# Dealing anew how many expert rows and routing heads stand beside each stage of a hybrid encoder layer

## The reference

```
proj = x @ w_in                       # q, k, v | latents of the second attention | two gates
o_a  = stick_breaking_attend(...)     # first attention ("stick"), 8 heads of 64
o_b  = mla_attend(...)                # second attention ("mla"), 8 heads
h = layer_norm(ALPHA * x + (sig(g_a) * (o_a @ w_oa) + sig(g_b) * (o_b @ w_ob)) @ w_out)
# PEER, for each token:
q = (h @ peer_wq).reshape(8 heads, 2, 128)
s1, i1 = top_k(q0 @ sub_keys0, 16);  s2, i2 = top_k(q1 @ sub_keys1, 16)
top_s, experts = top_k(s1[:, None] + s2[None, :], 16)      # out of 16384 experts
ff = sum over 8 heads x 16 picks of  softmax(top_s) * gelu(u[e] . h) * v[e]
y = layer_norm(ALPHA * h + ff)
```

## Time and profile before

| | |
|---|---|
| median of 3 runs | 3386.64 us |
| profiled execution, and its span | 3386.37 us, 3384.6 us |
| TensorE (PE) matmul busy | 2957.3 us, 87% |
| VectorE (DVE) busy | 2398.4 us, 71% |
| GpSimd (POOL) busy | 1548.0 us, 46% |
| ScalarE (ACT) busy | 1204.6 us, 36% |
| DMA | 1096.91 MB, mean 324 GB/s |

### The profile page before, as it was taken

One profiled execution on the slowest core, in us unless ns is written; L12 is line 12 of the kernel. 1 busy time (PEld: TensorE's weight loads), 2 busy tenths in 40 slices (PEclk: granted clock), 3 DMA queues, 4 the chain that ended last, 5 costly groups with the idle time before them and its releaser, 6 DMA issues. The chain is left out here.

```text
span 3384.6 us, 35758 instructions
## 1 busy us (share of the span) xinstructions
PE 2957.3 (87%) x10191; PEld 1649.7 (49%) x10191; DVE 2398.4 (71%) x4846; ACT 1204.6 (36%) x3117; POOL 1548.0 (46%) x1180
## 2 busy tenths in 40 slices
PE   8989989766697998876788899999989999999993
PEld 5755655443444555433444555544444545545551
DVE  0121477787777867887767777777778787888887
ACT  0241233474633434775653332222222222322221
POOL 0000066655664677876878643323333333333330
PEclk9978999887798999897799999999999999999996
DMA  4566699868699999557689999999999999999994
GB/s 148 192 247 203 215 337 336 310 220 273 226 357 389 385 337 348 157 176 221 173 280 329 334 388 416 415 415 415 415 416 415 415 414 415 410 408 413 415 407 178
DMA packets 374853, 1096.91 MB, mean 324 GB/s; under 512 B 91616, under 2 KB 209344, under 8 KB 288512
## 3 DMA queue, kind: packets, MB, share of 16 engines
q0 software_dynamic: 164784, 750.26, 58.7%
q1 hardware_dynamic: 176800, 303.85, 25.3%
q10 hardware_dynamic: 33072, 40.51, 3.4%
HBM read 1031.18 MB, written 62.23 MB: 323 GB/s over the span
## 5 line engine op out<-in xcount | busy, mean ns | idle before, releaser
L459 POOL DMA_INDIRECT expert_rows<-in_experts,picked_index x525 | 620.7, 1182 | 881.9 <-DVE ff_sum L613 756.2
L601 DVE SCALAR_TENSOR_TENSOR expert_rows<-expert_rows,h_tile 128x1024 f32<-128x1024 f32 x557 | 679.3, 1220 | 236.1 <-DMA expert_rows<-in_experts,picked_index 217.6
L482 POOL DMA_INDIRECT gates_by_expert<-dense_gate,gate_address x384 | 680.7, 1773 | 164.0 <-issue 116.5
L1829 PE MATMUL dense_out_ps<-dense_value_rows,dense_weights 128*128 128x512 f32 x1536 | 697.1, 604 | 63.4 <-DVE dense_weights L1907 63.4
L613 DVE SCALAR_TENSOR_TENSOR ff_sum<-expert_rows,coefficients,ff_sum 128x1024 f32<-128x1024 f32 x557 | 712.9, 1280 | 29.3 <-ACT coefficients L564 28.1
L1840 PE MATMUL dense_act_ps<-dense_hT,key_columns 128*128 128x384 f32 x2048 | 683.1, 487 | 5.8 <-issue 3.5
L1840 PEld LDWEIGHTS dense_act_ps<-dense_hT,key_columns 128*128 128x128 f32 x2048 | 389.1, 190 | 306.7 <-issue 55.9
L1829 PEld LDWEIGHTS dense_out_ps<-dense_value_rows,dense_weights 128*128 128x128 f32 x1536 | 294.8, 193 | 422.7 <-issue 314.7
L870 PE MATMUL proj_ps<-xT,w_in_block 128*128 128x384 f32 (+1 forms) x1392 | 421.8, 466 | 29.2 <-PEq L1640 16.1
L558 ACT ACTIVATE activated<-dots 128x1 f32<-128x1 f32 (+1 forms) x629 | 125.9, 200 | 883.6 <-DVE expert_rows L601 653.1
L870 PEld LDWEIGHTS proj_ps<-xT,w_in_block 128*128 128x128 f32 x1392 | 268.0, 193 | 182.4 <-issue 35.6
(11 more groups left out here) (199 smaller groups left out, 3228.2 us busy)
## 6 DMA issues: line engine op xcount, KB each, us to landing
key_columns<-in_key_columns SPq DMA_DIRECT2D x128, 512.0 KB
dense_value_rows<-in_experts SPq DMA_DIRECT2D x128, 512.0 KB
gates_by_expert<-zeros POOLq DMA_DIRECT2D x12, 2048.0 KB, 21.9
wq_half<-in_peer_wq SPq DMA_DIRECT2D x48, 512.0 KB
dense_gates<-gates_by_expert SPq DMA_DIRECT2D x128, 192.0 KB
w_in_block<-in_w_in ACTq DMA_DIRECT2D x18, 1024.0 KB
w_in_block<-in_w_in SPq DMA_DIRECT2D x18, 1024.0 KB
w_out<-in_w_out SPq DMA_DIRECT2D x24, 512.0 KB, 7.2
```

The lines of the kernel that those rows point to most:

```text
L459: pool.indirect_dma_start(to, None, self.a["experts"], bass.IndirectOffsetOnAxis(ap=index[:, k:k + 1], axis=0)).then_inc(got, 16)
L482: pool.indirect_dma_start(self.a["gates_by_expert"], bass.IndirectOffsetOnAxis(ap=self.flat[i][:, k:k + 1], axis=0), self.dgate[i][:, k:k ...
L601: dve.scalar_tensor_tensor(place, place, 1.0, self.h[n % 2][:], ALU.mult, ALU.mult, accum_out=self.dots[:, s % TOPK:s % TOPK + 1]).then_in ...
L1829: mm = nc.tensor.matmul(out[d][:, 512 * half:512 * (half + 1)], w[e % AB][:, P * d:P * (d + 1)], vals[e % VB][:, 512 * half:512 * (half + ...
```

## The change

Only the numbers of `SHARES` change. The work of the program as a whole is the same: 689 row steps, 66 heads of routing, 384 scatters.

```diff
-        ((1, "project"), 44, 1, 7, 44), ((1, "stick"), 24, 2, 2, 24), ((1, "mla_project"), 8, 1, 1, 10), ((1, "mla"), 22, 2, 2, 24),
-        ((1, "merge"), 22, 1, 0, 20), ((1, "scores"), 27, 1, 3, 16),
-        ((2, "project"), 39, 1, 8, 56), ((2, "stick"), 28, 2, 5, 60), ((2, "mla_project"), 7, 1, 1, 20), ((2, "mla"), 25, 2, 5, 56),
-        ((2, "merge"), 16, 1, 2, 34), ((2, "scores"), 28, 1, 3, 30),
+        ((1, "project"), 36, 1, 9, 50), ((1, "stick"), 29, 2, 0, 30), ((1, "mla_project"), 10, 1, 0, 10), ((1, "mla"), 22, 2, 2, 24),
+        ((1, "merge"), 22, 1, 1, 16), ((1, "scores"), 27, 1, 3, 16),
+        ((2, "project"), 34, 1, 11, 58), ((2, "stick"), 36, 2, 1, 58), ((2, "mla_project"), 7, 1, 1, 20), ((2, "mla"), 30, 2, 3, 54),
+        ((2, "merge"), 14, 1, 4, 34), ((2, "scores"), 26, 1, 4, 34),
```

## The result

| | before | after |
|---|---|---|
| median, same chip | 3385.57 us (9 runs, 3380.03 to 3390.80) | 3401.42 us (9 runs, 3394.80 to 3409.49) |
| ratio | | 1.0039, 95% interval 1.0029 to 1.0050 |
| profiled span | 3384.6 us | 3398.8 us |
| TensorE, VectorE, GpSimd busy | 2957.3, 2398.4, 1548.0 us | 2950.1, 2403.6, 1538.1 us |

The account below looks back on a forecast made before the run. Bounds were taken by block: TensorE and DMA in projections, GpSimd in stick 2 to mla 2, DMA in dense. Terms -8 -1 -1 +0 +1.5 +1 -4 +3.5 +2 -3 = -9 gave 3377.5 us; own range 3368 to 3384, overall 3352 to 3400.

Parts of the forecast that it names:

- The projections: Project 1 -8 us (-12 to -3), barrier wait 14.5 to some 6.5; project 2 +1 (-3 to +7).
- Stick 1: Stick 1, 5 rows more and 2 heads fewer: -1 us, between -5 and +4; VectorE +12 - 14.
- mla_project 1 at -1 and mla 1 at 0: mla_project 1: -1 us (-3 to +3); mla 1 keeps its shares: 0 (-2 to +2 together with scores 1).
- The three blocks -4: Stick 2, mla_project 2 and mla 2 together, bound by GpSimd: -4 us, between -12 and +6.
- its -3 for both blocks: GpSimd's work over stick 2 and mla 2, from fetches, scatters and score loads: about -3 us in all.
- VectorE's -11: VectorE's work: stick 2 -8.8 us and mla 2 -2, expected to be given back in good part.
- ScalarE's tables: Stick 2: gelu table loads taken as covered; the rival has them bind, +10.3 us on ScalarE's path, 3393 total; chance 0.04.
- Merge 2 at +3.5: Merge 2, 2 rows fewer and 2 heads more: +3.5 us, between 0 and +9; VectorE 4 late in the seventh step.
- Scores 2 at +2: Scores 2, 2 rows fewer and 1 head more around the wait for tile 5's scores: +2 us, -3 to +8.
- Dense at -3: Dense: 3 rows fewer -7.6 us, late scatters +5 (0 to +18); in all -3, between -8 and +10.
- The rival of the freeze: Dense: a stop of 25 us from late scatters isn't made up, dense +17, 3398 total; chance 0.12.
- GpSimd takes the attentions' gain: Rival: GpSimd's scatter backlog runs from stick 2 to mla 2, +5 us instead of -4, 3386.5 total; chance 0.08.

Follow-up runs that it names:

- e5_rows25: e3_even with 25 row steps in mla 2 in place of 30, dense taking the 5: 3386.98 us, ratio 0.9985.
- e9_rows_only: The changed kernel with 25 row steps in mla 2 in place of 30, heads kept, dense taking the 5: 3381.62 us, ratio 1.0000.
- e6_mlap: The changed kernel with mla_project 1's old shares (8 row steps, 1 head, the head taken from merge 1): 3398.36 us, ratio 1.0024.
- e11_two_fixes: The changed kernel with the edits of e6_mlap and e9_rows_only together: 3377.26 us, ratio 0.9977.
- e3_even: The changed kernel with group 2's same rows but its heads spread as 10, 4, 1, 4, 2, 3: 3401.10 us, ratio 1.0033.
- e10_scatters: e3_even with 42 scatters allowed in mla 2 in place of 54: 3397.73 us, ratio 1.0039.
- e4_gates: The changed kernel with 60 scatters allowed in scores 2 in place of 34, so none is left for dense: 3415.38 us, ratio 1.0071.
- e13_stick_rows: The changed kernel with 24 row steps in stick 1 in place of 29, dense taking the 5: 3385.09 us, ratio 1.0008.
- e8_combined: Against the changed kernel: group 1 as e6_mlap; group 2 keeps the new deal only in projection and stick: 3375.90 us, ratio 0.9966.
- e7_gates1: The changed kernel with group 1's old numbers of scatters allowed, rows and heads kept: 3394.05 us, ratio 1.0016.

## Why the prediction was wrong

The forecast was a sum of -9 with its steps by block; +14.2 came. By its own steps:

- **The projections: right.** -8 for project 1 and +1 for project 2, with the tail of one piece as what remains. TensorE's wait at the barrier fell from 14.5 to 6.7, where 6.5 was forecast, and project 2 kept its 6.6, with 8 us more of VectorE's work under its cover (152.4 busy against 144.0). After, in project 1:

```profile
634.60 3.79 PE L964 MATMUL log_weight_ps<-sb_qT,sb_kT 64*128 64x128 f32 x32 [6.70 <-PEq L720]
```

- **Stick 1: right in sign, small.** -1 against -4.4. Two heads were 9.2 us with 29 rows and 127.2 - 110.6 = 16.6 with 24, on either side of the forecast's 14; five rows were 4.8 and 12.2, where 12 stood.
- **mla_project 1 at -1 and mla 1 at 0: the first failed step.** They came at +5.3 and +9.5. A block with the same shares was priced by its shares. What it inherits was left out: where the heads' boundaries fall in GpSimd's queue, shown for mla 1, and the transfers in flight over the barrier, behind which the weights of mla_project 1 came 5.1 us late for a reason that stays open. Of the 23.2 us between forecast and result, 6.3 are mla_project 1 and 10.5 mla 1 with scores 1.
- **"The three blocks -4": the step that decided the sign.** Stick 2 was right (-6.4 within "3 to 8"), mla_project 2 -0.4, but mla 2 was +17.8 instead of about nothing. The forecast had the bound right (GpSimd, "never free") and then set its -3 for both blocks against VectorE's -11. It counted 3 us less for GpSimd over stick 2 and mla 2, and the busy time did come at the same (283.8 and 283.4 by the earlier trace rows and the windows above). But a block is bound by its own part of the queue and the places, and neither was priced: 5 rows in mla 2 are 17.6 and 20.2 us by e5_rows25 and e9_rows_only, 3.5 to 4 each (2.2 by e6_mlap against e11_two_fixes), where the forecast had 1.07 + 0.3. From e3_even to e5_rows25 half of it is the fetches (8.2 of 17.6) and half the scatters, of which fewer and faster ones ran in the block; in the changed kernel most of it is GpSimd's waiting for `ff_sum` (15.3 of 20.2), which the forecast had at nothing ("never free").
- **ScalarE's tables did not bind.** Stick 2 is shorter with 17 loads of the gelu table seen than with 14, at the same 1283 ns; the rival that gave them 10 us more on the path fell.
- **Merge 2 at +3.5: mis-sized.** +9.5. The new shares were worth 1.7 to 3.9 (no run over 4), as the forecast had it; the other 6 go with the run of 18. It had been priced for one step (4 us late) and taken as caught up afterwards. GpSimd's wait for `ff_sum` went to 33.3 us, from 6.7, but that alone says little: in e10_scatters it is 26.0 and the block is as short as in e3_even.
- **Scores 2 at +2: right by the number, wrong in the reason.** With the same shares the block was 13 to 15 us shorter than before where 13 or 14 rows stood ahead of tile 5's first head, and +1.1 with the 8 of this list. The forecast had named the wait (19.3 us until the scores of tile 5 have landed) and that the head ahead fills part of it, and it did fall to 13.8. It priced two rows fewer there as a small loss, and did not see what the place of that head is worth: five rows more ahead of it go with some 15 us less.
- **Dense at -3: right in mechanism.** -8.8. TensorE stopped as described, at its fifth iteration, for 11.2 us and not 15 to 25, and caught up. The late scatters cost 1.6 (after against e3_even), 6.6 (after against e4_gates) or 9.0 (e10_scatters against e3_even), where +5 stood; the blocks ahead differ in these pairs, so the size stays open. The row was probably too cheap: for five rows dense grew by 14.1 (e3_even to e5_rows25), 18.5 (after to e9_rows_only), 17.0 (after to e13_stick_rows) and 10.0 (e6_mlap to e11_two_fixes), 2.0 to 3.7 each in place of 2.5. The rival of the freeze would have given the right total for the wrong reason.

Of the rivals, "GpSimd takes the attentions' gain" named the right engine and block, at +5 in place of +11 for the three. Its condition, a backlog from stick 2, is not what the runs show: e9_rows_only keeps stick 2 whole and loses nothing in mla 2, and at the start of mla 2 GpSimd is 9 scatters behind the list, before as after. The text's own test, "wrong if mla 2 is over 6 us longer", was met.

What stays open: why five rows in mla 2 cost as much by waiting (changed kernel) as by a full queue (e3_even); what makes the weights of mla_project 1 late; what sets the length of the wait for a landing; and whether moving tile 5's first head alone moves scores 2.

## What to carry to other kernels

Price a move of background work in the block it goes to, by the engine whose queue is full there, and not by a sum over several blocks: five rows cost 5 to 12 us in stick 1, 10 to 19 in dense and 11 to 20 in mla 2, where GpSimd has little slack. Write out the order that the planner will give, and price its long runs, how much stands ahead of a step whose input the block has yet to make, and the waits that fall at block boundaries in blocks whose own shares don't change too, because in an in-order queue with a fixed number of buffers one wait moves, and is paid where it lands. When a deal gains in some blocks and loses in others, undo it block by block: e8_combined kept the gains and beat both kernels.

## What the hardware showed

At the wait in mla 1 of the changed kernel and at its counterpart in e7_gates1, GpSimd saw a scatter's landing 10.5 and 9.1 us after it stopped, with the DMA share down to 0.22 in the first. In thirteen kernels this wait in mla 1 was 8.0 to 10.5 us, and it was paid in the block's length. GpSimd's queue runs on over a barrier: 8 scatters ran after the start of dense where the list has 5. Loads of weights on SyncE's queue came 4 to 7 us late in mla_project 1 of twelve kernels, and 0.1 us or less in the other four. In dense TensorE lost 11 us in the first 100 and the block was still 8.8 us shorter than before, with the DMA engines at a share of 1.02 over those 100: the late scatters behind that stop cost 1.6 to 9.0 us by three comparisons.
